# Exchanging the halves of a rotary embedding by DMA instead of by ScalarE copies

## The chip, the cores and the metric

The kernel runs on one core of a Trainium2 chip. The metric is the device time of one execution in microseconds, from three runs. TensorE, VectorE, ScalarE and GpSimd are called PE, DVE, ACT and POOL in the rows; SP is the engine that only issues transfers here.

## The reference

Two transformer blocks run one after the other on 512 positions of 1024 channels. The first block has two layers, of which the first mixes with differential attention and the second with windowed grouped-query attention; each then has a gated feed-forward part and a gated embedding. The second block has a third attention, without rotation. The change touches only the first two attentions, and in them the rotary embedding of queries and keys:

```python
def apply_rope(x, cos, sin):
    xf = x.astype(jnp.float32)
    x1, x2 = jnp.split(xf, 2, axis=-1)
    c, s = cos[:, :, None, :], sin[:, :, None, :]
    return jnp.concatenate([x1 * c - x2 * s, x2 * c + x1 * s], axis=-1).astype(x.dtype)

q = apply_rope(q.reshape(B, S, 2 * H, d), cos, sin)      # first attention, d = 64
k = apply_rope(k.reshape(B, S, 2 * H, d), cos, sin)
s = jnp.einsum('bqhd,bkhd->bhqk', qb, k).astype(jnp.float32) * scale
```

A head has 64 channels, so `x1` and `x2` are 32 channels each. In the first attention all four blocks of 128 keys are read by every block of queries. In the second, block i of queries reads key blocks i-1 to i+1, with masks and a sink logit.

## The kernel before

Channels lie on the 128 partitions and the 512 positions on the free axis, so a projection tile of 128 channels holds two heads, and the partner of a channel is 32 partitions away. All matrices are float32; a product is made of three matmuls over a high and a low part of each operand, which the code calls `mm3`. Each weight slab of 128x1024 is fetched by SP into `raw` (two buffers), copied to `whi` by ACT (`high`, one L982 activation, four buffers) and subtracted from it by POOL (L487, two instructions) into `wlo`. A slab's `high` is issued by ACT in `used(stage, i, j)`, once the slab four earlier has been consumed.

An attention is a software pipeline of 32 steps `g`, four for each pair of heads, one for each block of 128 queries. It is written out by hand, once for each engine, and each engine runs its own list in order. In step `g`:

- PE: `scores` of a later step (g+1 in the first attention, g+2 in the second), a piece of the projection of a later pair (`project_qk`), `transposes(g)` of the probabilities, and at even g above 0 `outputs(g-1)`.
- DVE: `maxima` of the later step's scores, `normalise(g+1)`, `prob_low(g)`. `maxima` of the second attention ends in two instructions on 128x2 (L1592, L1596); `normalise` is what lets PE transpose; `prob_low` makes the low half of the transposed probabilities.
- ACT: `exps(g+1)`, `prob_high(g)`, and, where a pair ends, `evacuate`.

In the first attention (`kind` 1) the 14 tiles of stage `qk1` are projected in halves, one tile every two steps. In the second (`kind` 2) the 8 tiles of `kq2` are projected in thirds, in the steps with g % 4 of 1, 2 and 3; below, r is g % 4. A tile that is finished in step g is rotated around step g+1: ACT copies the halves crosswise out of PSUM (`swap_halves`, four instructions of 32x512, at the end of step g), DVE makes PSUM times cosine (L1563, which gives the PSUM bank back through `tile_free`), swapped times sine (L1564) and their sum (L1567), all three between `maxima` and `normalise` of step g+1. Then ACT takes the high part of the sum (`q_high`, L1081) and DVE the low part (`q_low`, L1571, in step g+2, behind `maxima`). PE's `scores` of the pair that needs the tile wait for `q_low` through `q_ready`. From its second tile on, all tiles of `kq2` go to the same PSUM bank, bank 0, so that `open_tile` of a tile waits for the cosine product of the tile before.

Two further pairs of tiles, `qk1a` and `kq2a`, are rotated ahead of each attention. The tables `rC` and `rS` hold cosine and signed sine, both times the norm's factor; the sign is negative for the first 32 channels of a head. SP's program is a loop that waits for POOL (`lo_ready`) and loads the next slab.

Of the kernel before, what the change touches and what calls it, by code (L numbers as in the profile page):

```python
# [29 lines left out]
ALU = mybir.AluOpType  # L30
# [15 lines left out]
RAWS = 2  # L46
# [29 lines left out]
SLAB0, BEFORE = {}, {}  # L76
# [111 lines left out]
def build(nc, xT, pT, posd, wts, par, con, lamd, outT):  # L188
    ctx = ExitStack()
    with ctx:  # L190
# [109 lines left out]
        vhi_ready, pad_ready = sem("vhi_ready"), sem("pad_ready")  # L300
        swap_ready, rope_ready, qhi_ready, q_ready = (
# [101 lines left out]
        BEGUN = {1: {}, 2: {-2: 0, -1: 1}, 3: {-2: 2, -1: 3}}  # L403
# [55 lines left out]
        @block.sync  # L459
        def _(sp):  # L460
            def load(s, slot, freed):
                if freed is not None:

                    sp.wait_ge(lo_ready, freed)
                sp.dma_start(raw[:, slot, :], wts[s]).then_inc(raw_ready[slot], 16)

            for s in range(4):
                load(s, s % RAWS, s - 1 if s >= RAWS else None)
            with sp.Fori(1, SLABS // 4) as i:
                for j in range(4):  # L470
                    load(4 * i + j, j % RAWS, 4 * i + j - 1)
            for m in range(KC):

                bank, before = tile_of("down2.2", m // 4, m % 4)
                sp.wait_ge(tile_free[bank], before + 2)
                sp.dma_start(outT[:, m, :], X[:, m, :]).then_inc(out_stored, 16)
            sp.wait_ge(out_stored, 16 * KC)
# [498 lines left out]
        def _(act):  # L976
# [89 lines left out]
            def swap_halves(stage, t, n):  # L1066

                if stage not in ("qk1a", "kq2a"):
                    used(stage, 0, t)
                bank, _ = tile_of(stage, 0, t)  # L1070
                if n >= 2:

                    act.wait_ge(rope_ready, n - 1)
                for to, of in ((0, 32), (32, 0), (64, 96), (96, 64)):
                    last = act.activation(swap[to:to + 32, n % 2, :], PS[of:of + 32, bank, :], ACT.Copy)
                last.then_inc(swap_ready, 1)
# [70 lines left out]
            def attention(kind):  # L1147
# [6 lines left out]
                for g in range(steps):  # L1154
                    begun, halfway = finished(kind, g - 1), finished(kind, g - 2)
                    if g + 1 < steps:
                        exps(kind, g + 1)
                    if kind == 3 and begun is not None:
                        head_square(begun)
# [3 lines left out]
                    if kind < 3 and begun is not None:  # L1163
                        q_high(*place_of(kind, begun))
# [16 lines left out]
                    if done is not None and kind < 3:  # L1181
                        swap_halves(PROJ[kind], done, place_of(kind, done)[0])
# [105 lines left out]
            swap_halves("qk1", 0, 2)  # L1288
            q_high(*place_of(1, 0))
# [20 lines left out]
            swap_halves("kq2", 0, QT0[2] + 2)  # L1310
            exps(2, 0)
            q_high(*place_of(2, 0))
            swap_halves("kq2", 1, QT0[2] + 3)
# [140 lines left out]
        def _(dve):  # L1454
# [98 lines left out]
            def rope(stage, t, n):  # L1553
# [4 lines left out]
                dve.wait_ge(swap_ready, n + 1)  # L1558
# [8 lines left out]
                tt(qraw[:, b, :], qraw[:, b, :], swap[:, b, :], ALU.add).then_inc(rope_ready, 1)  # L1567

# [93 lines left out]
            def attention(kind):  # L1662
# [8 lines left out]
                for g in range(steps):  # L1671
# [7 lines left out]
                    if kind < 3 and begun is not None:  # L1679
                        rope(PROJ[kind], begun, place_of(kind, begun)[0])  # L1680
# [17 lines left out]
                    if g + 1 < steps:  # L1698
                        normalise(kind, g + 1)
                    prob_low(kind, g)  # L1700
                    if kind == 2:
                        for c in OSPLIT.get(g, ()):
                            output_low(OA, c)
# [157 lines left out]
            rope("qk1", 0, 2)  # L1861
            q_low(*place_of(1, 0))
# [19 lines left out]
            values_low("v2", (0,), 256)  # L1882
            maxima(2, 0)
            rope("kq2", 0, QT0[2] + 2)
# [378 lines left out]
```

## Time and profile before

| | |
|---|---|
| Three runs | 2183.09 us median, 2181.43 to 2187.6 us |
| The profiled execution | 2183.27 us, of which the traced span is 2181.3 us |
| Busy share of the span | PE 95%, DVE 57%, ACT 45%, POOL 42% |
| Granted TensorE clock, mean | 0.977 of full speed |
| Transfers | 179.53 MB in 49923 packets, mean 82 GB/s |

The first attention stands in the trace from about 89 to 270 us, the second from about 786 to 947 us. In a profile of this kind the busy shares are averages over stages with different limits, so a stage has to be read by its own rows: which engine is idle there, what ended the idle time (shown in brackets at a row's end, as microseconds and the line of the releasing instruction), and what the granted clock was. 1.00 in the clock column is 2.4 GHz, 0.50 is 1.2 GHz.

### The profile page before, as it was taken

Reading aid. Unit: us, or ns where it says so; the run is one execution under the profiler, and the core shown is the slowest. Engines: PE = TensorE matmul, PEld = TensorE weight load, DVE = VectorE, ACT = ScalarE, POOL = GpSimd, SP = SyncE. Lnnn points to the kernel's source line nnn. Section 1 sums busy time; section 2 is a strip of 40 time slices with the busy share of each in tenths; the row PEclk is TensorE's granted clock in tenths of the full one; section 3 lists DMA queues with packets and bytes.
Section 4 is the critical chain, followed back from the end, with each engine's and each line's share of the span. In section 5 each row is a group of like instructions: output and inputs, shape, how many; then the busy total and the mean of one; then the engine's idle time right before and its main releaser. Section 6 shows DMA issues by size and latency. Waiting matters only on the chain. (4 is left out here: it accounts for less than half of the span.)

```text
span 2181.3 us, 28619 instructions
## 1 busy us (share of the span) xinstructions
PE 2081.8 (95%) x9896; PEld 1696.5 (78%) x9896; DVE 1251.8 (57%) x1830; ACT 975.4 (45%) x1546; POOL 912.7 (42%) x660
## 2 busy tenths in 40 slices
PE   6999899999999989899999999999979999999999
PEld 5777578888887877778888887777768688888887
DVE  7477756636265668866726357548779664313222
ACT  5577534524245466644524245434642434423222
POOL 4422034545545431134555456344105354445444
PEclk9999799999999989999999999999989999999999
DMA  4211022323223210012222323222102222332223
GB/s 152 78 49 49 20 66 96 100 97 96 97 97 112 82 58 30 30 49 94 99 97 96 100 93 116 87 78 78 40 11 97 77 87 96 97 97 96 96 97 106
DMA packets 49923, 179.53 MB, mean 82 GB/s; under 512 B 5536, under 2 KB 5792, under 8 KB 49824
## 3 DMA queue, kind: packets, MB, share of 16 engines
q1 hardware_dynamic: 48384, 174.09, 24.2%
q10 hardware_dynamic: 1440, 4.08, 0.5%
q8 instruction: 68, 1.11, 0.2%
q14 instruction: 31, 0.25, 0.0%
HBM read 176.05 MB, written 2.10 MB: 82 GB/s over the span
## 5 line engine op out<-in xcount | busy, mean ns | idle before, releaser
L487 POOL TENSOR_TENSOR wlo<-raw,whi 128x512 fp32r<-128x512 f32 x656 | 912.5, 1414 | 1254.2 <-ACT whi L982 1252.8
L495 PE MATMUL PS<-Bhi,whi 128*128 128x512 f32 x2368 | 936.9, 396 | 29.2 <-POOL wlo L487 14.9
L495 PE MATMUL PS<-Blo,whi 128*128 128x512 f32 x2368 | 926.8, 391 | 0.0
L495 PE MATMUL PS<-Bhi,wlo 128*128 128x512 f32 x2368 | 926.7, 391 | 0.0
L982 ACT ACTIVATE whi<-raw 128x1024 fp32r<-128x1024 f32 x328 | 345.8, 1057 | 591.8 <-PE PS L495 521.8
L495 PEld LDWEIGHTS PS<-Bhi,whi 128*128 128x128 f32 x2368 | 447.6, 189 | 139.8 <-issue 30.1
L495 PEld LDWEIGHTS PS<-Bhi,wlo 128*128 128x128 f32 x2368 | 447.4, 189 | 94.8
L495 PEld LDWEIGHTS PS<-Blo,whi 128*128 128x128 f32 x2368 | 448.0, 189 | 90.7 <-issue 0.5
L1465 DVE TENSOR_TENSOR AR<-PS,R 128x512 f32<-128x512 f32 x172 | 116.5, 689 | 241.0 <-PE PS L495 228.9
L1517 DVE TENSOR_TENSOR X<-X,PS 128x512 f32<-128x512 f32 x96 | 65.8, 687 | 232.6 <-PE PS L495 231.8
L1722 DVE SCALAR_TENSOR_TENSOR AR<-AR,par_sb 128x511 f32<-128x511 f32 x88 | 117.0, 1329 | 8.8 <-ACT AR L1205 8.8
L1220 ACT ACTIVATE Bhi<-AR 128x512 f32 x66 | 41.8, 633 | 166.7 <-DVE AR L1738 166.7
L1940 DVE SCALAR_TENSOR_TENSOR AR<-AR,par_sb 128x512 f32<-128x512 f32 x120 | 114.6, 1012 | 0.0
L1725 DVE SCALAR_TENSOR_TENSOR AR<-AR,par_sb 128x511 f32<-128x511 f32 x88 | 106.8, 1213 | 12.9 <-DVE AR L1722 2.9
L1095 ACT ACTIVATE AR<-PS,nmax 128x512 f32<-128x512 f32 (+3 forms) x160 | 93.3, 590 | 42.7 <-DVE nmax L1584 40.7
L1474 DVE SCALAR_TENSOR_TENSOR Blo<-X,par_sb,Bhi 128x512 fp32r<-128x512 f32 x56 | 65.1, 1163 | 40.2 <-ACT Bhi L1003 39.9
L1205 ACT ACTIVATE AR<-AR,par_sb 128x512 f32<-128x512 f32 x88 | 71.0, 807 | 38.5 <-DVE AR L1465 38.5
L1116 ACT ACTIVATE pthi<-PS 128x512 fp32r<-128x512 f32 (+3 forms) x128 | 56.6, 477 | 67.0 <-PE PS L719 66.0
L1481 DVE TENSOR_TENSOR acc<-acc,sq 128x512 f32<-128x512 f32 x64 | 85.1, 1330 | 0.0
L1742 DVE TENSOR_TENSOR Blo<-AR,Bhi 128x512 f32 x66 | 47.1, 714 | 61.5 <-ACT Bhi L1220 61.5
L719 PE MATMUL PS<-constR,AR 128*128 128x128 f32 x368 | 62.0, 300 | 18.6 <-DVE ptlo L1633 13.1
L719 PEld LDWEIGHTS PS<-constR,AR 128*128 128x128 f32 x368 | 46.8, 153 | 39.7 <-DVE AR L1625 17.2
(222 smaller groups left out, 2072.8 us busy)
## 6 DMA issues: line engine op xcount, KB each, us to landing
raw<-in_weights SPq DMA_DIRECT2D x328, 512.0 KB, 3.3
X<-in_xT ACTq DMA_DIRECT2D x4, 512.0 KB, 7.7
out<-X SPq DMA_DIRECT2D x8, 256.0 KB, 3.2
AR<-in_pT ACTq DMA_DIRECT2D x2, 512.0 KB, 3.9
par_sb<-in_parameters ACTq DMA_DIRECT2D x1, 322.0 KB, 4.5
AR<-in_positions ACTq DMA_DIRECT2D x1, 256.0 KB, 9.0
con_sb<-in_constants ACTq DMA_DIRECT2D x1, 206.5 KB, 8.8
AR<-in_lambdas ACTq DMA_DIRECT2D x1, 128.0 KB, 8.7
```

The lines of the kernel that those rows point to most:

```text
L487: ins = pool.tensor_tensor(wlo[:, j, c], raw[:, j % RAWS, c], f32(whi[:, j, c]), ALU.subtract)
L495: return pe.matmul(out, w, x, start=start, stop=stop)
L719: last = pe.transpose(PS[:, 2 + n % 2, k * P:k * P + P], source[:, k * P:k * P + P], ident)
L982: act.activation(whi[:, slot, :], raw[:, slot % RAWS, :], ACT.Copy)\
L1095: act.activation(probs(kind)[:, 2 * (g % 2) + s, 0:nb * P], PS[:, score_bank(kind, n), 0:nb * P], ACT.Exp, bias=nmax[:, n % 4:n % 4 + 1], ...
L1205: act.activation(cv[:, 2 * pair + u, :], us[:, 2 * pair + u, :], ACT.Identity, scale=conv_w[:, l, 1, u, bass.ds(q, 1)], bias=conv_w[:, l, ...
L1465: tt(out, PS[:, bank, :], R[:, :], ALU.mult).then_inc(tile_free[bank], 1)
L1481: tt(acc[:, :], acc[:, :], sq[:, slot, :], ALU.add).then_inc(sq_used, 1)
L1517: tt(X[:, m, :], X[:, m, :], PS[:, bank, :], ALU.add)\
L1722: own.step(stt(c[:, 1:T], x[:, 0:T - 1], conv_w[:, l, 0, u, bass.ds(q, 1)], c[:, 1:T], ALU.mult, ALU.add))
L1725: stt(c[:, 0:T - 1], x[:, 1:T], conv_w[:, l, 2, u, bass.ds(q, 1)], c[:, 0:T - 1], ALU.mult, ALU.add).then_inc(conv_done, 1)
L1940: ins = stt(out, src, k, out, ALU.mult, ALU.add)
```

## The change

The 22 tiles of `qk1` and `kq2` are no longer swapped by ACT. DVE first makes PSUM times signed sine in `qraw` (`rope_sin`), SP moves the halves of `qraw` crosswise to `swap` with four transfers of 32 partitions (64 KB each), and DVE then makes PSUM times cosine in `qraw`, which gives the bank back, and subtracts `swap` (`rope_add`). The difference is the old sum, since the sign of the sine belongs to the other half. The tiles `qk1a` and `kq2a` are rotated as before. The core of the diff:

```diff
+            def exchange(n):
+                sp.wait_ge(sin_ready, n - 1 if n < QT0[2] else n - 3)
+                sp.wait_ge(rope_ready, n - 1)
+                for to, of in ((0, 32), (32, 0), (64, 96), (96, 64)):
+                    sp.dma_start(swap[to:to + 32, n % 2, :], qraw[of:of + 32, n % 2, :])\
+                        .then_inc(exchanged[n % 2], 16)
+            ahead = {SLAB0["qk1"] + j + 6: j + 2 for j in range(NPROJ[1])}
+            ahead.update({SLAB0["kq2"] + j + 6: QT0[2] + 2 + j for j in range(NPROJ[2])})
...
+                        if s in ahead:
+                            exchange(ahead[s])
+                        load(s, s % RAWS, s - 1)
...
+                    if kind == 2 and halfway is not None:
+                        q_high(*place_of(2, halfway))
...
                     prob_high(kind, g)
-                    if kind < 3 and begun is not None:
-                        q_high(*place_of(kind, begun))
+                    if kind == 1 and begun is not None:
+                        q_high(*place_of(1, begun))
...
-                        swap_halves(PROJ[kind], done, place_of(kind, done)[0])
+                        used(PROJ[kind], 0, done)
...
+            def rope_sin(stage, t, n):
+                done(stage, 0, t)
+                bank, _ = tile_of(stage, 0, t)
+                dve.wait_ge(q_ready, n - 1)
+                dve.wait_ge(qhi_ready, n - 1)
+                tt(qraw[:, n % 2, :], PS[:, bank, :], rS, ALU.mult).then_inc(sin_ready, 1)
+            def rope_add(stage, t, n):
+                bank, before = tile_of(stage, 0, t)
+                b = n % 2
+                dve.wait_ge(exchanged[b], 64 * (n // 2 if n < QT0[2] else n // 2 - 1))
+                tt(qraw[:, b, :], PS[:, bank, :], rC, ALU.mult).then_inc(tile_free[bank], 1)
+                dve.wait_ge(tile_free[bank], before + 2)
+                tt(qraw[:, b, :], qraw[:, b, :], swap[:, b, :], ALU.subtract).then_inc(rope_ready, 1)
...
-                    if kind < 3 and begun is not None:
-                        rope(PROJ[kind], begun, place_of(kind, begun)[0])
...
                     if g + 1 < steps:
                         normalise(kind, g + 1)
+                    if kind == 1 and begun is not None:
+                        rope_add("qk1", begun, place_of(1, begun)[0])
                     prob_low(kind, g)
+                    if kind == 2 and begun is not None:
+                        rope_add("kq2", begun, place_of(2, begun)[0])
+                    if kind < 3 and finished(kind, g) is not None:
+                        t = finished(kind, g)
+                        rope_sin(PROJ[kind], t, place_of(kind, t)[0])
...
-            rope("qk1", 0, 2)
-            q_low(*place_of(1, 0))
+            rope_sin("qk1", 0, 2)
             attention(1)
...
             values_low("v2", (0,), 256)
+            rope_sin("kq2", 0, QT0[2] + 2)
             maxima(2, 0)
-            rope("kq2", 0, QT0[2] + 2)
+            rope_add("kq2", 0, QT0[2] + 2)
+            rope_sin("kq2", 1, QT0[2] + 3)
             attention(2)
```

On DVE in the second attention, around the end of a step with r = 3 and in the step with r = 0, the rows before are these (L1633 of r = 3, `maxima`, the three rotations, `normalise`, L1633 of r = 0):

```order
L1633 TENSOR_TENSOR ptlo<-PS,pthi 128x2x128 x2
L1581 TENSOR_REDUCE nmax<-PS 128x1 x2
L1592 TENSOR_TENSOR nmax<-nmax,nsink 128x2
L1596 TENSOR_TENSOR sdiff<-nmax,nsink 128x2
L1563 TENSOR_TENSOR AR<-PS,AR 128x512
L1564 TENSOR_TENSOR AR<-AR 128x512
L1567 TENSOR_TENSOR AR<-AR 128x512
L1610 TENSOR_TENSOR rsum<-rsum 128x2
L1621 RECIPROCAL rinv<-rsum 128x2
L1625 TENSOR_SCALAR AR<-AR,rinv 128x384 x2
L1633 TENSOR_TENSOR ptlo<-PS,pthi 128x2x128 x2
```

At the same place of the changed kernel DVE has these (L1674 is `prob_low`, L1599 the sine product, L1622 to L1637 `maxima`, L1651 to L1666 `normalise`, L1606 the cosine product, L1608 the difference):

```order
L1674 TENSOR_TENSOR ptlo<-PS,pthi 128x2x128 x2
L1599 TENSOR_TENSOR AR<-PS,AR 128x512
L1622 TENSOR_REDUCE nmax<-PS 128x1 x2
L1633 TENSOR_TENSOR nmax<-nmax,nsink 128x2
L1637 TENSOR_TENSOR sdiff<-nmax,nsink 128x2
L1651 TENSOR_TENSOR rsum<-rsum 128x2
L1662 RECIPROCAL rinv<-rsum 128x2
L1666 TENSOR_SCALAR AR<-AR,rinv 128x384 x2
L1674 TENSOR_TENSOR ptlo<-PS,pthi 128x2x128 x2
L1606 TENSOR_TENSOR AR<-PS,AR 128x512
L1608 TENSOR_TENSOR AR<-AR 128x512
```

The sine product has moved ahead of `maxima`, and the cosine product and the difference behind `prob_low`; the count is the same.

On ACT at the start of the first attention the rows before are these (L982 `high`, L1075 the four copies, L1081 `q_high`, L1095 `exps`, L1116 `prob_high`):

```order
L982 ACTIVATE whi<-raw 128x1024
L1075 ACTIVATE AR<-PS 32x512 x4
L1081 ACTIVATE qkhi<-AR 128x512
L1095 ACTIVATE AR,sum<-PS,nmax 128x512
L1095 ACTIVATE AR,rsum<-PS,nmax 128x512
L1116 ACTIVATE pthi<-PS 128x4x128
```

In the changed kernel they are these (L1007 `high`, L1118 `exps`, L1139 `prob_high`, L1104 `q_high`):

```order
L1007 ACTIVATE whi<-raw 128x1024
L1118 ACTIVATE AR,sum<-PS,nmax 128x512
L1118 ACTIVATE AR,rsum<-PS,nmax 128x512
L1139 ACTIVATE pthi<-PS 128x4x128
L1104 ACTIVATE qkhi<-AR 128x512
```

The copies are gone, and `q_high` of the first tile has moved behind `exps` and `prob_high`.

On SP the part of the program for the projections of an attention is now written out, four transfers and a load in turn:

```order
L477 DMA AR<-AR 32x512 x4
L466 DMA raw<-in_weights 128x1024
L477 DMA AR<-AR 32x512 x4
L466 DMA raw<-in_weights 128x1024
L477 DMA AR<-AR 32x512 x4
```

Before, the loads stood alone, in a loop over all slabs. The load behind the exchange of tile j is that of slab j+6 of the stage.

## Rows read from the trace of the kernel before

**Rows 1.** Busy time by stretch: us, busy of PE, PEld, DVE, ACT, POOL; PEclk, DMA, GB/s

```profile
180.00:200.00 20.00, 19.87 (x107) 14.49 (x106) 14.85 (x30) 16.58 (x34) 5.07 (x4) 1.00 0.14 43
880.00:900.00 20.00, 17.94 (x126) 14.84 (x124) 16.80 (x48) 12.86 (x38) 2.53 (x2) 1.00 0.11 40
```

**Rows 2.** PE alone, second attention: us, busy, PEclk, DMA share, GB/s

```profile
822.00:825.00 3.00, 3.00 (x13) 0.67 0.37 150
861.00:864.00 3.00, 3.00 (x11) 0.50 0.14 55
```

**Rows 3.** Timeline of DVE, one tile's rotation in the second attention

```profile
874.73 1.02 DVE L1581 TENSOR_REDUCE nmax<-PS 128x1 f32<-128x384 f32 x2
875.85 0.68 DVE L1592 TENSOR_TENSOR nmax<-nmax,nsink 128x2 f32<-128x2 f32 x1
876.57 1.20 DVE L1596 TENSOR_TENSOR sdiff<-nmax,nsink 128x2 f32<-128x2 f32 x1
877.70 0.68 DVE L1563 TENSOR_TENSOR AR<-PS,AR 128x512 f32<-128x512 f32 x1
...
879.62 0.15 DVE L1610 TENSOR_TENSOR rsum<-rsum 128x2 f32<-128x2 f32 x1
...
880.67 0.75 DVE L1633 TENSOR_TENSOR ptlo<-PS,pthi 128x256 fp32r<-128x256 f32 x2
881.34 0.74 DVE L1581 TENSOR_REDUCE nmax<-PS 128x1 f32<-128x256 f32 x2
...
882.38 0.16 DVE L1596 TENSOR_TENSOR sdiff<-nmax,nsink 128x2 f32<-128x2 f32 x1
882.46 0.68 DVE L1571 SCALAR_TENSOR_TENSOR qklo<-AR,qkhi 128x512 fp32r<-128x512 f32 x1
```

**Rows 4.** Timeline of ACT, then of POOL, the same tile

```profile
875.18 2.39 ACT L1075 ACTIVATE AR<-PS 32x512 f32<-32x512 f32 x4
...
875.23 2.53 POOL L487 TENSOR_TENSOR wlo<-raw,whi 128x512 fp32r<-128x512 f32 x2 [16.66 <-ACT whi L982]
```

**Rows 5.** Timeline of PE, the same tile

```profile
878.32 0.38 PE L495 MATMUL PS<-qkhi 64*128 64x256 f32 x1 [0.94 <-ACT AR L1095]
...
879.60 0.50 PE L495 MATMUL PS<-Bhi,whi 128*128 128x512 f32 x1
...
881.23 0.85 PE L719 MATMUL PS<-constR,AR 128*128 128x128 f32 x6
...
883.20 0.39 PE L495 MATMUL PS<-qkhi 64*128 64x256 f32 x2 [1.11 <-DVE qklo L1571]
```

**Rows 6.** Timeline of PE, the tile before, at the lower clock

```profile
860.41 0.67 PE L495 MATMUL PS<-Bhi,whi 128*128 128x512 f32 x1
...
863.01 1.30 PE L719 MATMUL PS<-constR,AR 128*128 128x128 f32 x6
```

**Rows 7.** Two loads back to back on SP; stores by SP, issue to landing

```profile
0.75 0.87 SPq L465 DMA_DIRECT2D raw<-in_weights  x2
...
DMA to landing us min/median/max: 2.0/3.2/4.6
```

**Rows 8.** Timeline of PE, the second steps of the first attention

```profile
94.73 0.49 PE L495 MATMUL PS<-qkhi 64*128 64x512 f32 x1 [1.42 <-ACT AR L1095]
```

**Rows 9.** Timeline of ACT, PE and DVE after the first attention's last tile

```profile
229.33 2.39 ACT L1075 ACTIVATE AR<-PS 32x512 f32<-32x512 f32 x4
...
232.57 0.49 PE L495 MATMUL PS<-qkhi 64*128 64x512 f32 x1 [1.68 <-ACT AR L1095]
...
237.19 3.33 DVE L1649 RECIPROCAL R<-acc 8x512 f32<-8x512 f32 x1
```

**Rows 10.** Timeline of DVE, then PE, the first steps of the second attention

```profile
800.70 0.69 DVE L1563 TENSOR_TENSOR AR<-PS,AR 128x512 f32<-128x512 f32 x1
...
801.54 0.76 PE L495 MATMUL PS<-Bhi,whi 128*128 128x512 f32 x1
...
806.82 0.39 PE L495 MATMUL PS<-qkhi 64*128 64x256 f32 x2 [0.59 <-DVE qklo L1571]
```

More of the change, by code:

```diff
@@ L300, in build @@
         vhi_ready, pad_ready = sem("vhi_ready"), sem("pad_ready")
+        sin_ready, exchanged = sem("sin_ready"), [sem(f"exchanged{n}") for n in range(2)]
         swap_ready, rope_ready, qhi_ready, q_ready = (
@@ L401, in build @@
         OSPLIT = {29: (0, 1, 2), 30: (3, 4), 31: (5, 6)}
-        BEGUN = {1: {}, 2: {-2: 0, -1: 1}, 3: {-2: 2, -1: 3}}
+        BEGUN = {1: {-1: 0}, 2: {-2: 0, -1: 1}, 3: {-2: 2, -1: 3}}
         NPROJ = {1: 14, 2: 8, 3: 8}
@@ L468, in _ @@
                 load(s, s % RAWS, s - 1 if s >= RAWS else None)
-            with sp.Fori(1, SLABS // 4) as i:
-                for j in range(4):
-                    load(4 * i + j, j % RAWS, 4 * i + j - 1)
+            def exchange(n):
[6 more added lines that the diff above has]
+            ahead.update({SLAB0["kq2"] + j + 6: QT0[2] + 2 + j for j in range(NPROJ[2])})
+            groups = sorted({s // 4 for s in ahead})
+            at = 1
+            while at < SLABS // 4:
+                if at in groups:
+                    for s in range(4 * at, 4 * at + 4):
+                        if s in ahead:
+                            exchange(ahead[s])
+                        load(s, s % RAWS, s - 1)
+                    at = at + 1
+                else:
+                    end = min([x for x in groups if x > at] + [SLABS // 4])
+                    with sp.Fori(at, end) as i:
+                        for j in range(4):
+                            load(4 * i + j, j % RAWS, 4 * i + j - 1)
+                    at = end
             for m in range(KC):
@@ L1066, in swap_halves @@
             def swap_halves(stage, t, n):
-                if stage not in ("qk1a", "kq2a"):
-                    used(stage, 0, t)
                 bank, _ = tile_of(stage, 0, t)
@@ L1287, in _ @@
             values("v1", (1,), 4, T)
-            swap_halves("qk1", 0, 2)
-            q_high(*place_of(1, 0))
+            used("qk1", 0, 0)
             attention(1)
@@ L1309, in _ @@
             values("v2", (0,), 0, 256)
-            swap_halves("kq2", 0, QT0[2] + 2)
+            used("kq2", 0, 0)
             exps(2, 0)
-            q_high(*place_of(2, 0))
-            swap_halves("kq2", 1, QT0[2] + 3)
+            used("kq2", 0, 1)
             attention(2)
@@ L1556, in rope @@
                 b = n % 2
-                dve.wait_ge(swap_ready, n + 1)
+                dve.wait_ge(swap_ready, n + 1 if n < 2 else n - QT0[2] + 3)
                 if n >= 2:
```

## The prediction

> **What bounds the kernel now.** I read the page first: PE is busy nearly all of the span, so a change on ACT, DVE and SP can pay only where PE stands still. Then I read busy time by stretch, because the two attentions have different limits. In the middle of the first, PE is busy 19.87 of 20 us [rows 1]: nothing that ACT or DVE gives up there can shorten it. In the second, PE is busy 17.94 of 20 us while DVE has 16.80 us of work [rows 1]; neither is full, so a chain that runs from engine to engine sets the pace. Third, the timeline of each engine over one rotated tile of the second attention, with the idle time before each instruction. It shows PE standing twice for each tile: 0.94 us for `exps`, which are late because the four copies (2.39 us) stand ahead of them on ACT, and 1.11 us for `q_low`, which ends a long unbroken row of DVE instructions [rows 3 to 5]. Fourth, the clock: in two of the five tiles that have a projection behind them the granted clock fell to the lower of its levels just behind these pauses (means of 0.67 and 0.50 in 3 us) [rows 2].
>
> **First attention.** The copies' 2.39 us on ACT leave 14 tiles, but PE waits for them in two places only. At the start, PE waits 1.42 us for `exps` of step 1 [rows 8]. They are late since DVE's `maxima` of that step stand behind the three rotations and `q_low`, which in turn stand behind ACT's copies. Now only the sine product stands ahead of these `maxima`; `exps` can be made as soon as the scores are there, and the cosine product is behind them. The wait goes: **-1.4 us** (bounds 0 and -1.4). After the last tile PE waits 1.68 us for `exps` behind the copies of 229.33 to 231.7 [rows 9]. These `exps` now come 2.39 us earlier, so this wait goes too. But `q_high` still waits for the difference, and ACT makes the root for the output norm behind it; DVE's long reciprocal waits for that root at 237.19 [rows 9]. The difference now comes after `normalise`, so only part of the 1.68 us reaches the reciprocal: I take **-1.3 us** (bounds -0.5 and -1.7). Between the two places the transfers lie behind a step of PE work of over 5 us, in which DVE has waits of its own; SP's load of slab j+6 has until the end of tile j+2. Both cost nothing as long as a landing takes less than such a step.
>
> **Landing of an exchange.** The trace has no transfer within the on-chip memory. SP issued two loads in 0.87 us, 0.44 each, so that the fourth transfer starts about 1.3 us after the first. Stores of 256 KB, four times the size of one, landed 2.0 us after issue at the least, 3.2 at the median, 4.6 at most [rows 7]. So all four are there 3.3 to 4.5 us after the sine product, 5.9 at the worst; I take 3.5, nearest to the least, since a transfer is small and nothing else is queued (the slab before was loaded a whole tile earlier, the next is asked for only when POOL is done).
>
> The page "DMA: Bandwidth & Descriptors" of the Trainium skill, section "Anatomy of one DMA", gives about 2.0 us fixed and bytes/436 GB/s, 0.15 us for 64 KB; and its "Rules for kernel authors" advise to coalesce and say that two transfers to disjoint halves serialize, which speaks against four small ones. By its figures the last would land near 3.5 to 4 us, an estimate from that page, and the sum would be the same; no row here shows such a transfer.
>
> **Second attention, one tile.** I replay the tile of [rows 3 to 5] in the new order. The three rotations held DVE from 877.70 to 879.62, 0.64 us each; `normalise` then takes 1.05, `prob_low` 0.67, `maxima` up to `q_low` 1.12, `q_low` 0.68 [rows 3].
>
> - The sine product takes 874.73 to 875.37, and `maxima` begin there. The two small instructions at their end took 0.68 and 1.20 us, against 0.16 us for the same L1596 at 882.38, and ended when POOL's two subtractions did, at 877.76 [rows 3, 4]. They start 0.64 later but stall until the same time: `maxima` end at 877.7, or at 878.1 if both fall behind POOL's second one.
> - `exps` start at 875.2, where the copies began [rows 4], and are ready. `normalise` to 878.75 (or 879.15), `prob_low` to 879.4 (879.8). The exchange has landed at 875.37 + 3.5 = 878.9: hidden by 0.5 to 0.9 us.
> - Cosine product to 880.05 (880.45), difference to 880.7 (881.1), `maxima` to 881.8 (882.2), `q_low` to 882.5 (882.9). Before, it ended at 883.14.
> - PE: the wait of 0.94 us goes, and the scores are made. But the projection needs bank 0, which the cosine product now gives back at 880.05 to 880.45; before, the projection ran at 879.60 [rows 5]. At full clock it and the transposes take 1.63 + 0.85 us, and end at 882.5 to 882.95. The next scores thus start at 882.6 to 883.0 instead of 883.20: a gain of 0.2 to 0.6, **-0.4 us**.
> - At the low clock they take 2.60 and 1.30 us [rows 6], and the scores start at 883.95 to 884.35: 0.8 to 1.2 later than before, **+1.0 us**. Before, the wait of 1.11 us was the cover for a low clock; it is gone.
>
> PE's pauses are now one of over 2 us rather than two of about 1. I take the low clock for three of the five tiles: 3 x 1.0 - 2 x 0.4 = **+2.2 us** (bounds -3.0 and +6.0). The last tile has no projection behind it: **-0.4 us**. ACT's `q_high`, moved to the next step, is behind `exps` that wait for nothing, and is done while DVE makes the next `maxima`; without them it would cost its own 0.6 us.
>
> **Start of the second attention.** Tile 1 is rotated in step 0: DVE's `q_low`, `normalise`, `prob_low` and cosine product (0.68 + 1.05 + 0.67 + 0.64) from 800.70 end at 803.7, so the projection that started at 801.54 starts at 803.7, at the low clock ends with its transposes 3.9 us later, at 807.6, against scores at 806.82 [rows 6, 10]: **+0.8 us** (bounds 0 and +1.5).
>
> **Sum.** -1.4 - 1.3 + 2.2 - 0.4 + 0.8 = -0.1 us on the profiled execution's 2183.27 us. That execution stands 0.2 us above the median, so I forecast 2183.0 us.
>
> **Rivals.**
> 1. *The clock holds.* For it: three of five tiles kept it with the same total of pauses. Then -1.4 - 1.3 - 5 x 0.4 - 0.4 + 0.8 = -4.3 us, with the better ends of all bounds about -8: 2175 to 2179 us.
> 2. *All waits for ACT come back.* 1.42 + 1.68 and 0.94 at six tiles, 8.7 us: 2174.5 us. Against it: bank 0, which comes 0.5 to 0.9 us later. For it: this price rests on my order of DVE's stalls behind POOL, and an earlier end of `maxima` would remove it.
> 3. *The exchange lands late* (slower). It stands ahead of the cosine product, so each us beyond 879.4 delays bank, difference and `q_low` of every tile. With 4.6 us for a landing it comes at 881.3, 1.5 to 1.9 us late; at six tiles 9 to 11 us: 2193 us. It decides, that is makes the kernel slower by over 6.5 us, from a landing of 5.2 us after the sine product on. Against it: the transfers are small and alone in their queue.
> 4. *The low clock at every tile* and longer than the replay has it: 5 x 1.2 + 1.5 - 2.7 gives +4.8, some 2186 to 2190 us.
>
> **How the numbers follow.** A difference of 0.3%, 6.5 us, is about what a measurement can tell from none. Forecast 0.45, within 4 us of its number; rival 1 0.15, rival 2 0.13, rival 3 0.14, rival 4 0.13. Faster: rival 2, a part of rival 1 and what I have not seen, 0.2. Slower: most of rival 3 and a part of rival 4, 0.18. The range leaves out the far ends of rivals 2 and 3: 2175.5 to 2191 us.
>
> **What would show it.** In the changed profile: no wait of PE for `exps` at the start of the first attention, and none behind its last tile; in the second attention no 0.94 us waits, but one of PE's projection for the cosine product, over 2 us, at each of tiles 2 to 6; the wait for `q_low` below 0.5 us; DVE's cosine product starting without idle time, its transfers landing 3.3 to 4.5 us after the sine product; more stretches at the lower clock between 820 and 910 us. A DVE that stands ahead of the cosine product would prove rival 3. The prediction is wrong if the landing is over 5 us, or if the clock behaves otherwise than in three of five tiles.

## The result, and the profile after it

The changed kernel takes 2193.52 us, the median of six runs (2184.6 to 2196.48), against 2182.14 us for the kernel before on the same chip (six runs, 2181.43 to 2187.6). The ratio of the runs is 1.0041 with a 95% interval of 1.0027 to 1.0056 (the two medians alone give 1.0052): slower by some 0.4 to 0.5%, and above the range of 2175.5 to 2191 us. The profiled execution took 2195.13 us, its span is 2193.1 us.

The pages first: ACT, which lost the copies, is busy 924.1 us, and PE, the bound, has a new wait among its longest. The first line is busy time, its share of the span and the number of instructions. The columns of the second are line, operation, count, busy us and mean ns of one, idle time before it, and what ended most of that.

```profile
PE 2084.6 (95%) x9896; PEld 1701.4 (78%) x9896; DVE 1254.2 (57%) x1830; ACT 924.1 (42%) x1458; POOL 912.6 (42%) x660
...
L520 PE MATMUL PS<-Bhi,whi 128*128 128x512 f32 x2368 | 939.4, 397 | 46.7 <-DVE AR L1606 16.9
```

L1606 is the cosine product. The two stretches of [rows 1], in the changed kernel (us, busy of PE, PEld, DVE, ACT, POOL, with the number of instructions; PEclk; DMA share, GB/s):

```profile
180.00:200.00 20.00, 20.00 (x111) 14.80 (x110) 16.53 (x32) 11.21 (x25) 5.07 (x4) 1.00 0.27 79
880.00:900.00 20.00, 17.62 (x120) 15.01 (x120) 15.60 (x45) 9.68 (x32) 2.53 (x2) 0.91 0.12 38
```

In the middle of the first attention PE does 111 matmuls where it did 107, though its busy time could rise by 0.13 us only; from 120 to 200 us it does 440 where it did 414. In the second it does 120 where it did 126, at a clock of 0.91 instead of 1.00. That window flatters the kernel before: of its four stretches of 20 us from 820 to 900 two stood at 1.00 and two at 0.91. In the changed kernel all four stand at 0.91.

One tile of the second attention on DVE, which answers to [rows 3]:

```profile
835.01 0.68 DVE L1599 TENSOR_TENSOR AR<-PS,AR 128x512 f32<-128x512 f32 x1
835.61 1.01 DVE L1622 TENSOR_REDUCE nmax<-PS 128x1 f32<-128x384 f32 x2
836.73 0.18 DVE L1633 TENSOR_TENSOR nmax<-nmax,nsink 128x2 f32<-128x2 f32 x1
836.94 1.21 DVE L1637 TENSOR_TENSOR sdiff<-nmax,nsink 128x2 f32<-128x2 f32 x1
...
839.12 0.74 DVE L1674 TENSOR_TENSOR ptlo<-PS,pthi 128x256 fp32r<-128x256 f32 x2
840.39 0.69 DVE L1606 TENSOR_TENSOR AR<-PS,AR 128x512 f32<-128x512 f32 x1 [0.53 <-DMA AR<-AR]
841.12 0.69 DVE L1608 TENSOR_TENSOR AR<-AR 128x512 f32<-128x512 f32 x1
```

L1599 is the sine product, L1608 the difference. PE behind it, which answers to [rows 5], and SP's issues of the exchange:

```profile
838.19 0.27 PE L520 MATMUL PS<-constS 64*128 64x128 f32 x2
841.23 0.47 PE L520 MATMUL PS<-Bhi,whi 128*128 128x512 f32 x1 [2.76 <-DVE AR L1606]
841.53 0.58 PE L520 MATMUL PS<-Blo,whi 128*128 128x512 f32 x1
841.91 0.63 PE L520 MATMUL PS<-Bhi,wlo 128*128 128x512 f32 x1
```

```profile
835.72 3.21 SPq L477 DMA_DIRECT2D AR<-AR  x4
```

The reader is to see a chain here. The sine product ends at 835.69. SP needs 3.21 us to issue four transfers, and the cosine product, which stands behind the wait for them on DVE, starts at 840.39, 4.70 us after the sine product's end; DVE stood 0.53 us. Only when it is done is bank 0 given back, and PE, whose next instruction in order needs the bank, has paused for 2.76 us. Behind the pause the matmuls take 0.63 us, not 0.39: the clock is at 1.2 GHz. That repeats at each of the five tiles, with pauses of 2.37 to 2.94 us. PE alone, in 3 us windows (us, busy, PEclk, DMA share, GB/s), which answers to [rows 2]; the windows behind the first two pauses, from 822 and 843, show 0.58 and 0.67:

```profile
861.00:864.00 3.00, 2.40 (x7) 0.68 0.38 150
...
882.00:885.00 3.00, 3.00 (x14) 0.59 0.07 27
903.00:906.00 3.00, 3.00 (x14) 0.50 0.00 0
```

**Where the time went.** I compared the start of the same instruction in the two profiled executions. The table has this for every kernel of the study: us later (+) or earlier (-) than in the first profile of before. The places are, as times of before: the 55th maximum of the first attention (235.39), the first residual add behind it (294.83), a maximum at each of two places of the second attention, four tiles apart (843.18 and 919.26), and the first residual adds behind the second and third attention (956.31 and 1784.05). What stands at 1784 stays to the end within 0.1 us.

| kernel | 235 | 295 | 843 | 919 | 956 | 1784 | ratio to before [95%] |
|---|---|---|---|---|---|---|---|
| changed | -7.07 | -5.28 | -1.45 | +3.19 | +7.01 | +11.78 | 1.0041 [1.0027, 1.0056] |
| first_only | -7.49 | -7.04 | -8.75 | -8.57 | -7.91 | -2.91 | 0.9985 [0.9971, 0.9999] |
| first_again | -6.81 | -8.50 | -6.08 | -5.70 | -3.03 | +3.46 | 0.9993 [0.9983, 1.0002] |
| second_only | -0.38 | -1.43 | -0.58 | +4.73 | +7.92 | +11.12 | 1.0048 [1.0030, 1.0067] |
| cos_early | -6.91 | -7.65 | -6.86 | -8.19 | -5.09 | +1.17 | 1.0001 [0.9987, 1.0015] |
| sub_ahead | -6.69 | -6.32 | -4.83 | +0.45 | +3.20 | +7.69 | 1.0020 [1.0007, 1.0033] |
| add_early | -7.05 | -8.58 | -4.24 | +0.99 | +4.37 | +8.93 | 1.0038 [1.0025, 1.0051] |
| busy_pause | -6.05 | -7.75 | -4.82 | -2.50 | +1.03 | +8.54 | 1.0029 [1.0016, 1.0041] |
| two_of_four | -7.21 | -6.87 | -4.06 | -3.91 | -0.62 | +3.90 | 1.0007 [0.9994, 1.0019] |
| copies_kept | +14.15 | +14.66 | +12.74 | +12.94 | +13.75 | +18.93 | 1.0100 [1.0083, 1.0117] |
| before_again | +0.09 | -2.70 | -3.21 | -3.24 | -3.28 | -1.58 | one run, 2181.73 us |
| before_late2 | -0.03 | -1.74 | -1.74 | -1.73 | -1.75 | +5.08 | one run, 2188.36 us |
| before_late5 | -0.03 | -0.01 | -0.02 | -0.03 | 0.00 | +10.26 | one run, 2193.52 us |

So the changed kernel gains 7 us in the first attention, loses 12 between its end and the second output projection, and another 5 in the third attention, whose code is the same in both. The second profile of before (before_again) tells how far such numbers can be trusted: 0.1 us at 235, up to 3.3 us behind it.

Not all of the 12 us is the second attention's own. 2.5 us went in the first feed-forward, whose code is unchanged, and 3.3 us between the last maximum of the second attention (934.96) and the first residual add. first_again, whose second attention is as before, lost 2.7 us at the same place, and in both the clock was low for longer there than in before (first_again: 0.68, 0.50 and 0.68 in the windows of 3 us from 936 on, before 1.00, 0.51 and 0.92). One window of PE in before, then in the changed kernel:

```profile
951.00:954.00 3.00, 3.00 (x14) 1.00 0.00 0
951.00:954.00 3.00, 3.00 (x10) 0.50 0.00 0
```

What is left for the second attention itself is 6.5 us.

### The profile page after: what moved, and what is told of

Same layout as the page of the kernel before. It is cut to its first block and busy times, and to the rows that moved or that the text cites. A ratio compares the mean times of both kernels' runs of the same rounds, so it can differ in the third digit from the quotient of the medians.

```text
span 2193.1 us, 28555 instructions
## 1 busy us (share of the span) xinstructions
PE 2084.6 (95%) x9896; PEld 1701.4 (78%) x9896; DVE 1254.2 (57%) x1830; ACT 924.1 (42%) x1458; POOL 912.6 (42%) x660
## 3 DMA queue, kind: packets, MB, share of 16 engines
q8 instruction: 68, 1.11, 0.2%
## 5 line engine op out<-in xcount | busy, mean ns | idle before, releaser
L1007 ACT ACTIVATE whi<-raw 128x1024 fp32r<-128x1024 f32 x328 | 346.0, 1057 | 596.5 <-PE PS L520 532.1
L1118 ACT ACTIVATE AR<-PS,nmax 128x512 f32<-128x512 f32 (+3 forms) x160 | 93.0, 589 | 45.7 <-DVE nmax L1625 40.3
L1139 ACT ACTIVATE pthi<-PS 128x512 fp32r<-128x512 f32 (+3 forms) x128 | 56.7, 478 | 86.9 <-PE PS L744 85.5
```

What stands on the lines that cost most here:

```text
L1007: act.activation(whi[:, slot, :], raw[:, slot % RAWS, :], ACT.Copy)\
L1118: act.activation(probs(kind)[:, 2 * (g % 2) + s, 0:nb * P], PS[:, score_bank(kind, n), 0:nb * P], ACT.Exp, bias=nmax[:, n % 4:n % 4 + 1], ...
```

## The experiments

**Which half does it.** Two kernels have the exchange in one attention each and the old code in the other (four copies by ACT, then DVE's three rotations in one row). A part of the edit of first_only:

```diff
-            ahead.update({SLAB0["kq2"] + j + 6: QT0[2] + 2 + j for j in range(NPROJ[2])})
...
-                    if kind == 2 and begun is not None:
-                        rope_add("kq2", begun, place_of(2, begun)[0])
-                    if kind < 3 and finished(kind, g) is not None:
+                    if kind == 1 and finished(kind, g) is not None:
```

> The exchange by transfers in the first attention alone; the second attention is written as before. My theory (the first attention gained 5 to 7 us, part of it in stalls that the busy time of PE did not show; the second lost them again) expects the residual adds of the first output projection 5 to 7 us earlier than before, the first maxima of the second attention some 2 to 5 us earlier, no waits of 2.4 to 3.2 us of PE for a cosine product there, and 2176 to 2180 us. The rival, that the lead of 7 us in the one profile of the changed kernel was luck of that execution and only the 2.7 us of the prediction are real, expects 2180 to 2182 us and a lead of 3 us at most.

Measured: 2180.07 us against 2183.74 (30 runs of before), 7.49 us ahead at 235. The time lies on the border of my two cases; the lead at 235 decides, and it is no luck of one execution.

> The exchange by transfers in the second attention alone; the first is written as before. My theory (all of the loss is made in the second attention, some 1.3 us a tile and the clock behind each pause) expects no lead at the first output projection, 9 to 13 us lost between the first maxima of the second attention and its output projection, six waits of PE of 2.4 to 3.2 us for the cosine product, and 2190 to 2196 us. The rival, that the loss came from clock phases in the third attention that have nothing to do with the change, expects 5 us or less lost by the second output projection and 2186 to 2189 us.

Measured: 2194.39 us, next to nothing gained at 235 (0.39 us), and 9.35 us lost between 294.83 and 956.31, 8.6 of it from the first maxima of the second attention on (I had 9 to 13). Six waits for the cosine product, 17.3 us together. The loss of the change is that of its second half.

**Exchange or bank.** The loss can come from the bank that is freed late, or from DVE's wait for the transfers. In cos_early the sine product goes to another buffer, so the cosine product need wait for nothing and can stand where the rotations stood.

```diff
+                out = sq if n > QT0[2] else qraw
+                tt(out[:, n % 2, :], PS[:, bank, :], rS, ALU.mult).then_inc(sin_ready, 1)
...
+                    if kind == 2 and begun is not None:
+                        rope_cos("kq2", begun, place_of(2, begun)[0])
```

> As the changed kernel, but in the second attention DVE writes the sine product to another buffer, from which the transfers read, and makes the cosine product where the three rotations stood before, between maxima and normalise, without a wait for the transfers; the difference stays behind the low halves. Bank 0 so comes free some 2 us earlier. If the late bank is the cause of the loss (theory 1), PE's waits of 2.4 to 3.2 us go, the clock of 820 to 920 us is at least that of before (0.94 to 1.00 rather than 0.91), the tiles take 19 us or less, and the kernel takes 2172 to 2178 us. If the late landing is the cause (theory 2: DVE stands for the exchange, and with it the difference, the low half and the next scores), the waits of DVE for the transfers stay at 0.5 to 0.7 us a tile, the next scores come as late as in the changed kernel, and the kernel takes 2188 us or more.

Measured: 2184.68 us. The pauses for the bank went from 2.76 to 0.42 us; what is left is one of 1.66 to 1.88 us for the low half, which was 1.11 us where it stood in the kernel before:

```profile
834.23 0.47 PE L521 MATMUL PS<-Bhi,whi 128*128 128x512 f32 x1 [0.42 <-DVE AR L1605]
838.38 0.39 PE L521 MATMUL PS<-qkhi 64*128 64x256 f32 x2 [1.88 <-DVE qklo L1619]
```

From 843 to 919 it gains 1.3 us, where the changed kernel loses 4.6. Between the residual adds at 664.97 and at 956.31, which hold the whole second attention, it loses nothing (0.2 us gained), where the changed kernel loses 9.8. So the bank, given back late because its product stood behind the transfers, is the cause; DVE waits for the transfers only once, at the start. The time that I gave (2172 to 2178 us) was still missed by 6.7 us. The clock fell at two of the five tiles, as in before (0.93 from 820 to 840, 1.00 from 860 to 900), and 6.3 us went in the third attention (below).

**Order of the last three pieces.** add_early puts the whole `rope_add` ahead of the low halves of probabilities; sub_ahead does this with the difference alone, on top of cos_early.

```diff
-                    prob_low(kind, g)
                     if kind == 2 and begun is not None:
                         rope_add("kq2", begun, place_of(2, begun)[0])
+                    prob_low(kind, g)
```

> As the changed kernel, but in the second attention cosine product and difference stand ahead of the low halves of probabilities. If the place behind the low halves delays bank 0 (theory 1 in its simple form), it comes up to 0.7 us earlier. But the exchange lands 4.5 to 4.9 us after the sine product whatever stands there, so I expect DVE to stand 1.1 to 1.4 us for the transfers in place of 0.5 to 0.7, the cosine product at the same time, PE's waits for it within 0.2 us of 2.4 to 3.2, the low halves 0.7 us later and the time the same or up to 3 us longer: 2192 to 2198 us. If landing is not what binds (rival), the waits of PE fall by 0.7 us each and the time to 2187 to 2190 us.

Measured: 2192.84 us, on the spot. Waits of DVE for the transfers of 1.10 to 1.55 us at tiles 2 to 6, PE's waits 2.67 to 3.11 (2.37 to 2.94 in the changed kernel). The place behind the low halves costs nothing: the transfers are not there before.

> As the kernel with the cosine product early and the sine product in a buffer of its own, but with the difference ahead of the low halves of probabilities, right behind normalise. There PE waits for the low half of the rotated tile (1.9 us a tile in that kernel), so a difference that is 0.67 us earlier should bring the next scores 0.3 to 0.6 us earlier, at six tiles 2 to 4 us, if the exchange has landed by then: it lands 4.7 us after the sine product and normalise ends some 5.2 us after it. Then 2180 to 2182.5 us. If it has not landed, or if the low halves of probabilities that are 0.6 us later are what PE's output products wait for, the time is that of the other, 2184.7 us, or up to 2 us more.

Measured: 2189.16 us, 4.5 us more than cos_early (4.1 by the ratios, whose intervals overlap a little; from 843 to 919 it loses 5.3 us where cos_early gains 1.3). The next scores wait less (1.31 us), but a new wait appears ahead of the transposes, which need the bank that the low halves free:

```profile
838.25 0.85 PE L745 MATMUL PS<-constR,AR 128*128 128x128 f32 x6 [0.81 <-DVE ptlo L1681]
840.41 0.40 PE L521 MATMUL PS<-qkhi 64*128 64x256 f32 x2 [1.31 <-DVE qklo L1619]
```

Two pauses, 4.0 and 4.7 us together in the four tiles from 830 to 910, against one of 6.9, and a clock of 0.91 in each 20 us from 820 to 900. That the low halves hold PE up was the second of my two cases, but it cost over 4 us and not 2.

**How much is the landing, how much the clock.** two_of_four issues two of the four transfers of each exchange of the second attention, and so also moves half the bytes.

> As the changed kernel, but in the second attention only the first two of the four transfers of an exchange are made (partitions 64 to 127 of the exchanged halves keep old values, so this part of the computation is left out). Issues stand 0.6 us apart, and one of them took 1.0 to 1.6 us, so the last landing comes 1.2 to 2.2 us earlier. If the landing ahead of the cosine product is the cause of the late bank (my theory), DVE no longer stands for the transfers, but normalise and the low halves still hold the cosine product until 4.1 us after the sine product: the bank comes 0.5 to 0.7 us earlier, PE's waits fall from 2.8 to about 2.2 us, and the kernel takes 2188 to 2191 us. If landing did not matter, the time is that of the changed kernel within 1 us.

```profile
837.79 0.68 DVE L1607 TENSOR_TENSOR AR<-PS,AR 128x512 f32<-128x512 f32 x1
...
838.62 0.47 PE L521 MATMUL PS<-Bhi,whi 128*128 128x512 f32 x1 [2.15 <-DVE AR L1607]
```

Measured: 2187.06 us, 6.5 us below the changed kernel by the medians (7.4 by the ratios, whose intervals lie apart) and 1 to 4 better than I said. DVE no longer stands; the cosine product starts 4.77 us after the sine product's start (833.02) instead of 5.38, PE waits 2.15 us, and from 843 to 919 it loses 0.15 us where the changed kernel loses 4.64. So the last 0.6 us of landing, that is the two later transfers, costs over 1 us a tile: itself, and the clock, which fell behind three of its five pauses and not behind all (0.93 from 820 to 880, not 0.91).

busy_pause leaves the chain as it is, and lets PE repeat the scores ahead of the pause.

```diff
+                    more = 5 if kind == 2 and qb == 3 and 3 < g < 24 else 0
+                    for k in range(more + 1):
+                        last = mm3(...)
```

> As the changed kernel, but in the second attention the nine score products of steps 7, 11, 15, 19 and 23 are made six times over (the last time for use), so that PE works through most of the pause of 2.4 to 3.2 us ahead of the projection; 5 x 0.46 = 2.3 us of added work in each, and the scores are not read before 3 us later. If the pause is what brings the low clock (rival 4's mechanism), PE's waits for the cosine product fall below 0.6 us, the clock of 820 to 920 us rises from 0.91 to 0.97 or more, the projections end 1 us earlier and the kernel gains 3 to 6 us on the changed one: 2187 to 2190 us. If the clock falls on its own schedule, it stays at 0.91 and the time within 1.5 us of the changed kernel's.

```profile
820.00:840.00 20.00, 20.00 (x154) 17.68 (x153) 15.72 (x45) 9.57 (x31) 2.53 (x2) 1.00 0.14 40
840.00:860.00 20.00, 20.00 (x156) 17.79 (x154) 15.65 (x47) 9.59 (x32) 2.53 (x2) 1.00 0.14 41
```

Measured: 2190.1 us, by the medians 3.4 less than the changed kernel (by the ratios 2.6), with more work done. The two intervals (1.0016 to 1.0041 and 1.0027 to 1.0056) overlap, so that the times alone can't tell the two kernels apart. The profile can: the clock is 1.00 in all windows from 820 to 900. The idle time is what lets the clock fall. The added work ran 3.4 us a tile rather than 2.3, longer than the pause: the projection starts 2.17 us after the cosine product (836.18 and 838.35), against 0.84 in the changed kernel, so 1.3 us were lost again. Even so, it loses 2.32 us from 843 to 919 and not 4.64, 0.6 us a tile less. I can't give all of this to the clock: in three of the four exchanges from 830 to 895 us SP issued in 2.41 us, and DVE stood for none of these three.

Side by side, the idle time of PE at a tile and the number of the five tiles at which the clock fell: 2.37 to 2.94 us in one pause, five (changed kernel); 2.24 to 2.68 us in three pauses of 0.41 to 1.31, five (sub_ahead); 2.15 us in one, three (two_of_four); 2.07 to 2.30 us in two, two (cos_early); one or two pauses of about 1 us, two (before); none, none (busy_pause). So it wasn't the length of a single pause that decided.

**What the first attention gained.** copies_kept is first_only with four copies by ACT of the old shape at the end of a step, into a buffer that nobody reads. They aren't quite the old ones: they stand ahead of the slab's `high`, where the old ones stood behind it, and take 2.55 us, not 2.39.

```diff
+                for to, of in ((0, 32), (32, 0), (64, 96), (96, 64)):
+                    act.activation(OA[to:to + 32, 7, :], cosT[of:of + 32, :], ACT.Copy)
```

> As the kernel with the exchange in the first attention alone (2180.1 us, 7.4 us ahead of the profile of before when the first attention ends), but ACT makes four copies of the old shape at the old place in the first attention, into a buffer that nobody reads (extra work, no step of the computation). If the gain of the middle of the first attention comes from ACT's 2.4 us a tile (theory: PE stood in stalls that its busy time hid, in steps in which ACT has most to do), the lead at the first residual adds falls from 7 to 8.6 us to 1 to 4 us and the kernel takes 2182 to 2184 us. If it comes from DVE's new order alone, the lead stays at 6 us or more.

```profile
180.00:200.00 20.00, 19.05 (x89) 13.67 (x89) 14.51 (x26) 14.10 (x28) 5.01 (x4) 1.00 0.21 56
```

Measured: 2204.42 us. Its lead did not shrink to 1 to 4 us, it became 14 us behind, 22 us worse than first_only. PE waits for `exps` ten times between 100 and 235 us, 0.41 to 0.51 us each, and does 89 matmuls in 20 us. So the gain needs ACT's relief, and DVE's new order by itself gives none: with copies in place it is worse than the old one. ACT's `q_high` waits 2.9 us for the difference there, with `exps` behind it, which the old order did not have; so these 22 us are no measure of what the copies cost in the kernel before, and what ACT's relief would bring without DVE's new order was not run. The theory is right in direction, its size was missed by far.

**Is the gain of the first half real?**

> The kernel with the exchange in the first attention alone, once more (it took 2180.1 us against 2183.7 in the first comparison, ratio 0.9985 with an interval of 0.9971 to 0.9999). If its gain is real, the ratio comes out at 0.998 to 0.999 again, with an interval that lies below 1.0, and its stages stand as before: 7 us ahead at the first residual adds and 8 us at the second. If the first comparison was luck, the ratio is 0.9995 to 1.001.

Measured: 2182.53 us, ratio 0.9993 [0.9983, 1.0002]. Between my two cases. Its profiled execution (2186.64 us) is the slowest of its eleven. The lead at 295 is there again (8.50 us), but 1.6 us went at 430, 1.6 at 810, 2.7 at the second output projection and 6.5 in the third attention, all in unchanged code. By the medians the two comparisons give 3.7 and 1.5 us; the second alone can't tell it from none.

**The third attention.** All nine kernels with the exchange in the first attention lost 4.5 to 7.6 us there against the first profile of before. Three more profiles of before, one plain and two delayed, test whether the exchange has part in it.

> The kernel before once more, for the stages of a second profiled execution. If the 3 to 6 us that every changed kernel lost against the one profile of before in the third attention (unchanged code) come from that one execution's luck with the clock, this profile shows such a shift against the first too, at a place where nothing changed; if before keeps within 1 us at every stage, those 3 to 6 us follow from the change.

It shows +1.7 us from 1328 to 1784, 1.3 of it after 1738; the loss that the others share, at 1541 to 1584, isn't there.

```diff
+                    for _ in range(3 if stage == "o2" and j == 0 and k == 0 else 0):
+                        mm3(out, whi[:, slot, 0:P], wlo[:, slot, 0:P], hi[:, 0, :], lo[:, 0, :],
+                            True, True)
```

> The kernel before, with three products of three matmuls added at the head of the second output projection (each is 3 x 0.23 = 0.68 us, extra work without use): everything behind comes 1 to 2 us later. Seven kernels with the exchange in the first attention lost 4.6 to 7.5 us against both profiles of before in the third attention, whose code is the same, because the low clock behind 1488 us lasted 4.2 to 5.1 us rather than 3.3 and the clock fell again at 1529. If the moment of arrival decides that, this kernel (or the next) shows the same loss of some 5 us between the third and the fourth output projection. If not, both stand at a constant distance to before from the second projection to the end, and the loss is tied to the exchange in a way that I have not found.

> The same with seven products, 3.5 to 4.8 us later. By the moment of arrival, one of the two at least loses some 5 us in the third attention; otherwise both keep their distance to before within 1.5 us.

The added work makes them 2.1 and 4.8 us late. Then, in the third attention, they lose another 4.7 and 5.5 us, at the places where the changed kernels do. The same matmuls in before_again and, 2 us of added work earlier in the program, in before_late2 (PE, 3 us windows):

```profile
1528.00:1531.00 3.00, 2.13 (x20) 1.00 0.00 0
1531.00:1534.00 3.00, 2.58 (x23) 1.00 0.00 0
1534.00:1537.00 3.00, 3.00 (x23) 1.00 0.00 0
```

```profile
1531.00:1534.00 3.00, 2.10 (x16) 1.00 0.07 26
1534.00:1537.00 3.00, 2.57 (x26) 0.61 0.00 0
1537.00:1540.00 3.00, 3.00 (x12) 0.50 0.00 0
```

The kernel before loses the same 5 us without any exchange; it is the granted clock that makes the difference. That the moment of arrival decides it is the likely reading, not a proven one: there is one profile of each kernel, and why before_again, 3.3 us early (1.7 us lost), and second_only, 8.4 us late (2.7 us lost), were spared, I can't say.

## Why the prediction was wrong

**The middle of the first attention: failed.** "Nothing that ACT or DVE gives up there can shorten it" rested on PE busy 19.87 of 20 us [rows 1]. It was wrong by 4.6 us (from -2.50 us at 126 to -7.07 at 235; first_only and first_again show the same, before_again keeps within 0.1 us). The end of a matmul is modelled in these profiles, so that short stalls need not show as idle time; the count of instructions, 414 against 440 from 120 to 200 us, shows them. copies_kept takes all of the gain back and more, so it doesn't come without ACT's relief (16.58 us of work in 20 before, 11.21 now); which wait of PE was shortened at each step the trace can't show.

**Start of the first attention: right, too small.** The wait of 1.42 us [rows 8] is gone; 2.5 us were won by 126 us, above my bound of 1.4. The prediction had no term for the clock here, and in the kernel before it fell behind that wait, which it doesn't in the changed one. The same window in before and in the changed kernel:

```profile
96.00:99.00 3.00, 3.00 (x8) 0.50 0.02 5
96.00:99.00 3.00, 3.00 (x17) 1.00 0.27 66
```

How the 2.5 us divide between the wait, the clock and stalls that don't show, no run tells.

**End of the first attention: failed.** I let the wait of 1.68 us [rows 9] go with the copies, for -1.3 us. It became 2.44 us. `exps` aren't behind the copies alone: ACT's rows show what else stands there.

```profile
227.83 0.63 ACT L1104 ACTIVATE qkhi<-AR 128x512 fp32r<-128x512 f32 x1 [2.78 <-DVE AR L1608]
228.48 1.28 ACT L1161 ACT_TABLE_LOAD   x1
229.78 0.59 ACT L1161 ACTIVATE acc<-PS 8x512 f32<-8x512 f32 x1
230.38 1.28 ACT L1118 ACT_TABLE_LOAD   x1
231.68 0.69 ACT L1118 ACTIVATE AR<-PS,nmax 128x512 f32<-128x512 f32 x1
```

`q_high` waits for the difference, and the root with its two table loads, 3.15 us, stands between it and `exps`. I had followed the later difference to the reciprocal, and not to `exps`, which are behind the same `q_high` on ACT. In the kernel before, root and table loads stood behind these `exps` and ahead of the next, for which PE waited 1.33 us at 238.56; it now waits 0.89 there, so a part of that wait has only moved forward. In sum the end gave next to nothing: the lead was 6.5 us at 218 and 6.7 us at 262.

**Landing: mis-sized, and it carried the argument.** I took 3.5 us after the sine product, within 3.3 to 4.5, and it was 4.7 in the tile shown. The landing after issue was right (2.0 us at the median, the same as the smallest store of [rows 7]); the issues were not. I spaced them by 0.44 us, a half of the 0.87 us of [rows 7], so that the fourth starts 1.3 us after the first; they take 0.59 us each, and in each of tiles 2 to 6 one took 1.0 to 1.6. The line is the 88 issues, min/median/max in ns, first and last start:

```profile
L477 SPq DMA_DIRECT2D AR<-AR x88: 507/590/1626, 87.1 to 918.9; - x88
...
DMA to landing us min/median/max: 1.9/2.0/3.1
```

The exchange was not hidden by 0.5 to 0.9 us but late by 0.5 to 0.7 in four of five tiles. That is rival 3 begun, and rival 4 with it: I had worked out each by itself, with 5.2 us as the landing from which the first decides. That threshold was too high, since with the longer idle time the low clock came at every tile. The Trainium skill, page "DMA: Bandwidth & Descriptors", section "Rules for kernel authors", advises to coalesce many small transfers into one large one. No run here moves the same bytes in one transfer: two_of_four, over 1 us a tile cheaper, also moves half of them.

The prediction also takes about 2.0 us of fixed cost from that page; the section, "Anatomy of one DMA" in the Trainium skill, gives it for transfers that GpSimd issues. The transfers here are issued by SP. They landed 2.0 us after their issue too, so that the figure did no harm. What was missing beside it was the time of the issues.

**One tile of the second attention: right in kind, wrong in size and count.** The waits for `exps` and for `q_low` went and one for the cosine product took their place, as the replay had it. I gave -0.4 us at the full clock and +1.0 at the low one, in three tiles of five. The low clock came behind all five pauses, and a tile costs 1.16 us on average from 843 to 919 (4.64 in four): the price of a low-clock tile was nearly right, the number of such tiles was not. Filling the pause (busy_pause) kept the clock up in all of them.

**The sum.** I had -0.1 us. Measured in stages: -7.1 to 235 us where I had -2.7 with the end; +1.8 to 295 us; +2.5 in the first feed-forward; +6.5 in the second attention to its last maximum, where I had +2.6; +3.3 from there to the first residual add; +4.8 from there to 1784, that is in the third attention. I had nothing for what lies outside the two attentions.

So three steps of the prediction failed. The middle of the first attention, put at nothing, gave 4.6 us. The second attention, with a late exchange and the low clock at every tile, cost 3.9 us more than I said. These two nearly cancel. What makes the time miss is a term that isn't in the sum: the stages behind a change whose code is the same in both (2.5, 3.3 and 4.8 us of the places above, 10.6 together). The prediction let them only move. In the two that I looked at, at 951 and behind 1530 us, the granted clock is lower than in before.

The medians contain this too: the profiled executions of before and of the changed kernel stand within 2 us of theirs, and second_only lies 11 us above before by its median, with 6.3 us lost in the second attention itself. How much of it would come out otherwise at another moment of arrival, one profile of each kernel can't say.

**Does a better version follow?** Of the kernels that I ran, the exchange in the first attention alone is the best, 0.07 and 0.15% below before in two comparisons, which is at the edge of what can be measured.

## What to carry to other kernels

Before work is moved behind a transfer on an in-order engine, ask what that work gives back: here a product that needed nothing from the transfer freed a PSUM bank for TensorE, and a landing 0.6 us later turned into 1.1 us a tile, in part through the clock. If a destination of its own separates the two, do that first (cos_early took back all of the second attention's loss, though in time it only equals the kernel before). And an engine that reads as 99% busy with modelled ends needn't be full: compare instruction counts per stretch, and look on the engine that feeds it for every instruction behind the one whose releaser comes later.

## What was not expected of the hardware

- **The issue of a small transfer between on-chip buffers** took SP 0.59 us at the median and up to 1.63 us, and landed 2.0 us after it (64 KB). In the changed kernel one issue of four took 1.0 us or more in each of tiles 2 to 6 of the second attention. During each of these the trace has a packet of an instruction queue, and during only 5 of the 82 issues under 0.9 us; no run tests whether that is the cause.
- **More work, no more time.** 3.4 us of useless matmuls a tile held the clock at 1.00, and the kernel was no slower for it: 3.4 us faster by the medians, which is within the noise.
- **Unchanged code moves by 5 us.** With a delay of 2.1 us at one projection the one profile taken is 6.8 us later at the end, because the clock falls at 1534 us, some 580 us later, where it had held in both plain profiles of before.
